# The last expert block's results kept in SBUF and added in the mix through a slot-by-token matrix

## The chip, the cores and the metric

One NeuronCore of one Trainium2 chip runs the whole program; its kernel is written in Bass, with an instruction stream of its own for each of TensorE (PE), VectorE (DVE), ScalarE (ACT), GpSimd (POOL) and SyncE (SP), tied together by semaphores. The metric is the device time of one execution in microseconds, the median over several runs.

## What is computed

Two layers of a diffusion backbone over 256 context tokens and 512 latent tokens of width 1024. Each layer mixes tokens (latent attention, Fourier mixing, neighbourhood attention) and then runs a hierarchical mixture of experts, in float32. The change touches the second part only:

```python
def hier_moe(h, w_rg, b_rg, w_re, b_re, w_gate, w_up, w_down):
    p_grp = jax.nn.softmax((h @ w_rg + b_rg).astype(jnp.float32), axis=-1)
    p_top, g_idx = lax.top_k(p_grp, 1)                      # 1 of 4 groups
    ...
    l_top, e_loc = lax.top_k(e_in, TOP_K)                   # 2 of its 8 experts
    w_tok = (p_top * jax.nn.softmax(l_top, axis=-1)).astype(h.dtype)
    ...
    def expert_block(args):
        xblk, e = args
        return (jax.nn.silu(xblk @ w_gate[e]) * (xblk @ w_up[e])) @ w_down[e]
    yb = lax.map(expert_block, (xb, block_e)).reshape(n_rows, d)
    out = jnp.zeros((t + 1, d), yb.dtype).at[row_tok].add(yb * row_w[:, None])
```

The result goes, scaled by a modulation row, into `ALPHA * x + out` and a layer norm. The first layer does this for 768 tokens (6 tiles of 128), the last one for the 512 latent tokens (4 tiles).

## The kernel before, in words

`NB` = 19 expert blocks of up to 128 slots (a slot is a pair of token and choice) are run in each layer in an order fixed by `expert_blocks` (L150 on). A block serves one expert, two (64 slots each) or four (32 each); which expert stands at which rank is computed on the chip (`of_rank`, `eord`). Blocks 17 and 18, the last two, serve two experts each. `expert_plan` makes a list of steps of it: `rows` (the block's token rows are turned, L1243), `gate`, `up` and `down` in two halves each (`product`, L1230), and `mid` (the product of gate and up is turned, L1253). The last steps are gate 18, mid 17, gate 18, up 18, down 17 (both halves), mid 18, down 18 (both halves).

Expert weights come in packs of 2 MB into `RAW` = 8 slots of SBUF (`raw`). `weight_packs` cuts them: a pack is one whole matrix of one expert, or, where `in_halves` says so, the same half of two experts' matrices. `in_halves` is true for the last block's down weights: pack 94 is the first half of both experts, pack 95 the second, while packs 92 and 93 are the whole down matrices of block 17's two experts, and both are needed before its first half product. A layer has 96 packs. SP issues them in order (L3010), each as soon as the last product that used its slot is done. Behind them on SP's queue stand the rows of the norm (`ln_g`, `ln_b`, in layer 0 two modulation rows as well), which wait for pack 92 to be used.

A block's result lies in PSUM (`slot[1]`); ACT copies it (layer 0, L2513), or DVE scales it (layer 1, L2110), into `yb[i % 2]`, and POOL writes its rows with an indirect DMA to `y_rows` in DRAM (`result`, L2711), one row for each pair of token and choice. When the last two blocks' stores have landed (`y_stored`), POOL raises `y_out`, and SP loads the two rows of each token, tile by tile, into `yg` (L3088); `yg[0]` lies over `yb`. The mix (L700) is then a product with a diagonal matrix for each of the two choices (`share[n][k]` = identity times the token's weight):

```python
for half in range(2):
    for k in range(2):
        last = pe.matmul(slot[n % 2][:, half * 512:(half + 1) * 512], share[n][k],
                         yg[n % 4][k][:, half * 512:(half + 1) * 512], start=(k == 0), stop=(k == 1))
```

A float32 `matmul` leaves two records on PE in the trace. In layer 1 the mix of 4 tiles is followed on DVE by `last_sum` (L1410), the moments, `last_centre` and `last_scale`, and by the output DMAs. In layer 0 tiles 0 to 3 are mixed behind the experts, and tiles 4 and 5 among the first projections of layer 1; DVE goes from `merge_first` (L1379) through `merge_last` to the next norm, and PE turns the normed tiles (L821) and multiplies (L772).

Ahead of the experts DVE computes each pair's slot. `place[k]` (L2044) is a matrix of tokens by slots for choice k that is one where the token's pair has that slot in its block.

`cst` holds constants, its last 1536 columns the position tables (`C_COS`, `C_SIN`), loaded once.

Of the kernel before, what the change touches and what calls it, by code (L numbers as in the profile page):

```python
# [70 lines left out]
C_KCOL, C_RANK, C_HALF, C_CAP, C_ALL, C_NEXT = (C_KROW + NE + k for k in range(6))  # L71
C_BLOCK = C_NEXT + 1
# [20 lines left out]
def shape_constants():  # L93
# [21 lines left out]
    c[:NE, C_NEXT] = np.where(e < DOUBLE, P * e - P, 0)  # L115
    b = np.where(e < hot, e, np.where(pair, hot + (e - hot) // 2, hot + PAIRED // 2 + (e - cold) // 4))
# [93 lines left out]
def program(nc, a, out):  # L210
# [9 lines left out]
    with ExitStack() as ctx:  # L220
# [49 lines left out]
        rk = sb("rk", [P, 464])  # L270
# [110 lines left out]
        idsT = rk[0:NE, 336:464]  # L381
# [20 lines left out]
        yg = [[ar(kb, D), ar(kb + 4, D)] for kb in (128, 136, 144, 80)]  # L402
# [244 lines left out]

        def blocks_to(L, i):

            return sum(1 for k in range(NB) if k % 2 == i % 2) * L + i // 2 + 1  # L650
# [10 lines left out]
        def _(pe):  # L661
# [31 lines left out]
            def mix(L, n):  # L693
# [134 lines left out]
            for L in range(DEPTH):  # L828
# [65 lines left out]
                def latent_value(t):  # L894
                    pe.wait_ge(act_taken, mark["latent", L, t])
                    if t == 0:
                        pe.wait_ge(mla_in, 16 * (NLATER + NMLA * (L + 1)))
# [270 lines left out]
                for k in range(2):  # L1168
                    pe.wait_ge(route_p, 4 * L + k + 1)
# [14 lines left out]
                for k, at in enumerate((C_HALF, C_CAP, C_ALL, C_NEXT)):  # L1184
                    pe.matmul(ps[:, 32 + 32 * k:64 + 32 * k], cst[0:NE, at:at + 1].to_broadcast([NE, P]), of_rank,
                              start=True, stop=True)
                close(pe.matmul(ps[0:NE, 160:161], of_rank, cst[0:NE, C_ALL:C_ALL + 1], start=True, stop=True), vgroups)

                def ranked_ids():

                    ps = vec()
                    for k in range(2):
                        pe.wait_ge(route_p, 4 * L + k + 3)
                        for n in range(nq):
# [9 lines left out]
                                    cst[0:NE, C_TOP + NE:C_TOP + 2 * NE], start=True, stop=True), vgroups)  # L1204

# [71 lines left out]
                for step in plan:  # L1277
                    part, i, half = step
                    if part == "rows":
                        rows_turned(i)  # L1280
                        if i == 1:
                            ranked_ids()
                    elif part == "mid":
# [59 lines left out]
        def _(dve):  # L1343
# [150 lines left out]
            for L in range(DEPTH):  # L1494
# [94 lines left out]
                dve.wait_ge(mla_in, 16 * (NLATER + NMLA * (L + 1)))  # L1589
# [416 lines left out]
                dve.tensor_copy(rk[:, 128:256], ps[:, 32:160])  # L2006
                dve.tensor_tensor(xe[0:NE, 1:2], xe[0:NE, 2:3], ps[0:NE, 160:161], ALU.subtract).then_inc(vec_taken, 1)
# [33 lines left out]
                for k in range(2):  # L2041
# [3 lines left out]
                    dve.sem_inc(route_p, 1)  # L2045

# [41 lines left out]
                for step in plan:  # L2088
# [3 lines left out]
                    if part in ("gate", "up") and half == 1:  # L2092
# [5 lines left out]
                        else:  # L2098
# [3 lines left out]
                                          ).then_inc(half_taken, 1)  # L2102
                    if part == "down" and half == 1 and L + 1 == DEPTH:
# [4 lines left out]
                        if blocks_to(L, i) > 1:  # L2108
                            dve.wait_ge(y_stored[i % 2], 16 * (blocks_to(L, i) - 1))
# [7 lines left out]
                def extra_block(j, b, it):  # L2117
                    with dve.If(count > j):
# [12 lines left out]
                        if L + 1 == DEPTH:  # L2131
                            put = dve.tensor_tensor(yb[0], slot[1][:, :], gf_row, ALU.mult)
                        else:
                            put = dve.tensor_copy(yb[0], slot[1][:, :])
# [6 lines left out]
                if L + 1 < DEPTH:  # L2141
                    dve.wait_ge(unit_used, mark["part_done", L, NB - 1, "down"])
                    shares()
# [14 lines left out]
        def _(act):  # L2158
# [16 lines left out]
            for L in range(DEPTH):  # L2175
# [67 lines left out]
                for c, (name, dst, blocks) in enumerate((("f", fT, qb), ("nq", nqT, qb), ("nk", nkT, BLOCKS))):  # L2243
                    hi = f_hi if name == "f" else n_hi
                    for m in range(4):
# [13 lines left out]
                        if name == "nk" and m:  # L2259
                            if m == 1:  # L2260
                                act.wait_ge(mla_in, 16 * (NLATER + NMLA * (L + 1)))
# [232 lines left out]
                for part, i, half in plan:  # L2494
                    if part == "rows":
                        ps = take()
                        act.copy(xT[i % 3][:, 4:KD, :].rearrange("p a b -> p (a b)"), ps[:, :]).then_inc(act_taken, 1)  # L2497
                    elif part == "mid":
# [624 lines left out]
```

## Time and profile before

| | us |
|---|---|
| median of 3 runs | 2656.22 |
| lowest and highest | 2653.99, 2663.89 |
| the profiled execution's own time | 2657.63 |
| its span | 2655.7 |
| PE busy (matmul) | 2451.5 |
| DVE, ACT, POOL busy | 940.9, 662.8, 352.8 |

Times in the trace are microseconds from the start of the span. A busy PE is not PE at its peak: matmuls are pipelined. "issue" in a chain is time in which an engine waited for nothing that the profile shows. The granted clock (PEclk) is 1.00 at 2.4 GHz and 0.50 at 1.2 GHz.

### The profile page before, as it was taken

The page shows a single profiled execution, that of the slowest core. Times are in us where ns is not written, and L with a number is a line of the kernel's source. Part 1 is how long each engine was busy: PE and PEld are TensorE (multiplying, and loading weights), DVE is VectorE, ACT ScalarE, POOL GpSimd, SP SyncE. Part 2 cuts the span into 40 slices and gives each one's busy share as a digit, 9 for nine tenths or more (in the row PEclk, how much of TensorE's full clock was granted, in tenths as well). Part 3 has the DMA queues.
Part 4 walks back from the last instruction along what each step waited for, and adds up shares of the span by engine and source line. Part 5 has one row for each costly group of instructions (what it writes and reads, how often), then busy time and mean ns, then how long its engine had stood idle before and what let it go on. Part 6 is the DMA issues. An engine that isn't in the chain of part 4 may idle for free.

```text
span 2655.7 us, 32991 instructions
## 1 busy us (share of the span) xinstructions
PE 2451.5 (92%) x12867; PEld 1553.1 (58%) x12867; DVE 940.9 (35%) x1791; ACT 662.8 (25%) x1242; POOL 352.8 (13%) x404
## 2 busy tenths in 40 slices
PE   7999999999999888999996999999999898999995
PEld 4768666788888633443332668567888633443332
DVE  3335466622225720000003544566334730111113
ACT  3221345632222210111011521456333200000000
POOL 1241000000112220010001531000011220010002
PEclk9999999999999889999997999999999889999997
DMA  8671000322214599999998471003433799999995
GB/s 283 213 258 48 7 1 12 75 65 69 65 56 166 226 415 423 427 422 425 427 428 308 158 239 48 7 1 74 113 97 110 299 383 424 426 421 425 427 427 196
DMA packets 217916, 603.87 MB, mean 227 GB/s; under 512 B 63280, under 2 KB 139472, under 8 KB 184736
## 3 DMA queue, kind: packets, MB, share of 16 engines
q1 hardware_dynamic: 189794, 526.02, 51.7%
q0 software_dynamic: 24512, 63.13, 6.8%
q10 hardware_dynamic: 3456, 12.58, 1.2%
q8 instruction: 108, 1.77, 0.3%
q14 instruction: 46, 0.38, 0.0%
HBM read 585.17 MB, written 38.16 MB: 235 GB/s over the span
## 4 chain that ended last, share of the span: by engine, by line
PE 72%; DMA 14%; DVE 7%; ACT 3%; issue 3%; POOL 1%; SPq 1%; DVEq 0%; ACTq 0%; POOLq 0%
PE slot L1230 23%; PE abank L772 18%; PE vbank L772 10%; DMA arena<-in_w_up_e 5%; DMA arena<-in_w_down_e 5%; PE slot L955 2%; PE vbank L989 1%; PE vbank L936 1%; DMA arena<-in_w_in 1%; PE slot L1016 1%; PE abank L872 1%; PE slot L700 1%; PE vbank L762 1%; PE vbank L1049 1%; PE abank L969 1%
## 5 line engine op out<-in xcount | busy, mean ns | idle before, releaser
L1230 PE MATMUL slot<-arena 128*64 128x512 f32 (+2 forms) x3264 | 827.3, 616 | 70.5 <-DMA arena<-in_w_up_e 47.6
L1230 PEld LDWEIGHTS slot<-arena 128*64 128x64 f32 (+2 forms) x3264 | 298.1, 147 | 546.3 <-issue 536.2
L772 PE MATMUL abank<-round,round 128*128 128x512 f32 (+1 forms) x1792 | 493.2, 356 | 9.4 <-DVE round L1501 3.7
L772 PEld LDWEIGHTS abank<-round,round 128*128 128x128 f32 x1792 | 318.7, 189 | 73.1 <-issue 15.9
L772 PE MATMUL abank<-hT_low,round 128*128 128x512 f32 (+1 forms) x896 | 318.1, 355 | 0.0
L772 PE MATMUL vbank<-round,round 128*128 128x512 f32 (+3 forms) x1248 | 290.0, 361 | 6.3 <-issue 5.1
L2101 DVE TENSOR_TENSOR arena<-slot,arena 128x512 f32<-128x512 f32 x76 | 52.6, 692 | 657.3 <-ACT arena L2506 377.9
L772 PEld LDWEIGHTS vbank<-round,round 128*128 128x128 f32 x1248 | 215.4, 189 | 41.0 <-issue 8.3
L772 PEld LDWEIGHTS abank<-hT_low,round 128*128 128x128 f32 x896 | 169.0, 189 | 24.0 <-issue 0.5
L1809 DVE TENSOR_TENSOR arena<-vbank,arena 128x512 f32<-128x512 f32 x72 | 43.4, 603 | 291.9 <-PE vbank L772 284.5
L2683 POOL TENSOR_TENSOR arena<-arena 128x512 f32<-128x512 f32 (+1 forms) x48 | 55.9, 1165 | 578.6 <-DVE arena L1809 578.6
L2497 ACT COPY arena<-abank 128x512 f32<-128x512 f32 x38 | 22.3, 586 | 375.8 <-PE abank L1243 375.7
L2434 ACT ACTIVATE arena<-abank,bT 128x512 f32<-128x512 f32 x72 | 44.5, 619 | 272.7 <-PE abank L772 272.7
L955 PE MATMUL slot<-arena 96*128 96x256 f32 (+1 forms) x288 | 102.7, 475 | 3.5 <-ACT arena L2318 1.8
L1713 DVE TENSOR_TENSOR round<-arena,round 128x1536 fp32r<-128x1536 f32 x48 | 89.5, 1865 | 46.1 <-ACT round L2343 46.1
L2705 POOL DMA_INDIRECT arena<-h_rows,ids x34 | 34.8, 1024 | 487.8 <-PE abank L1243 371.8
L772 PE MATMUL slot<-round,round 128*128 128x512 f32 x384 | 91.4, 400 | 0.4 <-DVE round L1781 0.4
L2343 ACT CAST round<-arena 128x1536 fp32r<-128x1536 f32 x48 | 71.1, 1480 | 63.5 <-PE vbank L772 63.5
L2502 ACT COPY arena<-abank 128x512 f32<-128x512 f32 x38 | 21.9, 587 | 254.3 <-PE abank L1253 254.3
L772 PEld LDWEIGHTS slot<-round,round 128*128 128x128 f32 x384 | 74.2, 194 | 16.6 <-issue 0.8
L2326 ACT ACTIVATE arena<-slot,nmx 128x768 f32<-128x768 f32 (+1 forms) x80 | 65.2, 817 | 64.4 <-DVE nmx L1690 64.4
L2711 POOL DMA_INDIRECT y_rows<-arena,ids x34 | 33.9, 997 | 332.4 <-DVE arena L2110 168.8
(335 smaller groups left out, 2862.4 us busy)
## 6 DMA issues: line engine op xcount, KB each, us to landing
arena<-in_w_up_e SPq DMA_DIRECT2D x44, 2048.0 KB, 25.1
arena<-in_w_down_e SPq DMA_DIRECT2D x44, 2048.0 KB, 26.0
arena<-in_w_gate_e SPq DMA_DIRECT2D x40, 2048.0 KB, 26.9
arena<-in_w_gate_e SPq DMA_DIRECT2D x48, 1024.0 KB, 15.2
arena<-in_w_ada POOLq DMA_DIRECT2D x80, 512.0 KB, 5.0
arena<-in_w_up_e SPq DMA_DIRECT2D x40, 1024.0 KB, 17.8
arena<-in_w_down_e SPq DMA_DIRECT2D x40, 1024.0 KB, 30.8
arena<-in_w_in SPq DMA_DIRECT2D x48, 512.0 KB, 4.3
```

Of the source, the lines that this page charges most:

```text
L772: last = pe.matmul(to, x, y, start=(k == 0 and q == 0), stop=(k == len(terms) - 1 and q == 2))
L955: last = pe.matmul(s[:, o:o + nn], qT[h % 2][0:QK, t * P:(t + 1) * P], kT[h % 4][0:QK, o:o + nn], start=True, stop=True)
L1230: last = pe.matmul(to[at, cols], x[:, at], w[:, at_w, :], start=first, stop=final)
L1713: dve.tensor_tensor(gate_halves(u)[1], graw[u % GRAW], gate_halves(u)[0].bitcast(F32), ALU.subtract).then_inc(w_lower, 1)
L1809: dve.tensor_tensor(dst, ps[:, 0:nn], sg[n % 2][:, 0:nn], ALU.mult).then_inc(vec_taken, 1)
L2101: dve.tensor_tensor(am[i % 3], slot[0][:, n % 2 * FE:n % 2 * FE + FE], am[i % 3], ALU.mult).then_inc(half_taken, 1)
L2326: act.activation(PR[i % 2][:, 0:nk], slot[(ib + i) % 2][:, 0:nk], ACT.Exp, bias=nmx[:, k:k + 1], scale=1.0, accum_out=rsum[:, k:k + 1]).th ...
L2343: act.copy(gate_halves(u)[0], graw[u % GRAW]).then_inc(w_upper, 1)
L2434: act.activation(sg[n % 2][:, 0:nn], ps[:, 0:nn], ACT.Sigmoid, bias=bT[:, col:col + 1], scale=1.0).then_inc(act_taken, 1)
L2683: pool.tensor_tensor(dst, dst, sg[n % 2][:, 0:nn], ALU.add).then_inc(pool_sum, 1)
L2705: pool.indirect_dma_start(out=xb[i % 2], out_offset=None, in_=h_d[:, :], in_offset=names(i), bounds_check=2 * TOK - 1, oob_is_err=False).t ...
L2711: pool.indirect_dma_start(out=y_d[:, :], out_offset=names(i), in_=yb[i % 2], in_offset=None, bounds_check=2 * TOK - 1, oob_is_err=False).t ...
```

## The change

1. `in_halves` now holds for the down weights of the last two blocks: pack 92 is the first half of both of block 17's experts, pack 93 the second.
2. Block 18's result is not stored. Its share in the mix is a third product for each half of a tile: `last_at[:, n, :]`, a matrix of 128 slots by 128 tokens that holds a token's weight at its slot of block 18, times `yb[0]`. `yg` moves off `yb`.
3. The matrix is made after the places: DVE finds the pairs whose expert stands in the last block and whose slot lies in it, multiplies their weight into `last_by` and takes it out of `wtok`; PE turns `last_by` (`last_turned`), ACT copies it. Both lie over the position tables, which SP reloads at the start of layer 1.
4. Rows of `y_rows` that no block writes any more are zeroed once, in layer 0, by a DMA from a zeroed row.
5. SP and POOL wait for the stores of blocks 16 and 17; `shares` (DVE, layer 0) comes ahead of block 18's end; extra blocks (none run with these inputs) use `yb[1]`.

```diff
 def in_halves(order, i, part):
     wide = len(order[i][1]) == 4
-    return wide or i == 0 and part != "down" or i == 1 and part == "gate" or i == len(order) - 1 and part == "down"
+    return wide or i == 0 and part != "down" or i == 1 and part == "gate" or i >= len(order) - 2 and part == "down"
...
+        last_at, last_by = (cst[:, o:o + TOK].rearrange("p (a b) -> p a b", a=NTILES) for o in (C_COS, C_SIN))
+        zero_row = ar(168, 256)
...
-        yg = [[ar(kb, D), ar(kb + 4, D)] for kb in (128, 136, 144, 80)]
+        yg = [[ar(kb, D), ar(kb + 4, D)] for kb in (136, 144, 80, 96)]
...
                 if n >= 2:
                     pe.wait_ge(t_ready, before(L) + n - 1)
-                for half in range(2):
+                elif n == 1:
+                    pe.wait_ge(y_ready, NB * (L + 1))
+                halves = [slice(half * 512, (half + 1) * 512) for half in range(2)]
+                for at in halves:
                     for k in range(2):
-                        last = pe.matmul(slot[n % 2][:, half * 512:(half + 1) * 512], share[n][k],
-                                         yg[n % 4][k][:, half * 512:(half + 1) * 512], start=(k == 0), stop=(k == 1))
+                        pe.matmul(slot[n % 2][:, at], share[n][k], yg[n % 4][k][:, at], start=(k == 0), stop=False)
+                if n == 0:
+                    pe.wait_ge(y_ready, NB * (L + 1))
+                for at in halves:
+                    last = pe.matmul(slot[n % 2][:, at], last_at[:, n, :], yb[0][:, at], start=False, stop=True)
                 last.then_inc(mixed, 1)
...
+                pe.matmul(ps[:, 192:224], cst[0:NE, C_LAST:C_LAST + 1].to_broadcast([NE, P]), of_rank, start=True, stop=True)
...
+                def last_turned():
+
+                    pe.wait_ge(route_p, 5 * L + 5)
+                    for lo in range(0, nq, 4):
+                        ps = act()
+                        for n in range(lo, min(lo + 4, nq)):
+                            last = pe.transpose(ps[:, (n - lo) * P:(n - lo + 1) * P], last_by[:, n, :], ident)
+                        close(last, agroups)
...
+                dve.tensor_copy(last_row, ps[:, 192:224])
...
+                link(dve.scalar_tensor_tensor(sel, q32b, 1.0, each(last_row), ALU.is_lt, ALU.mult))
+                for k in range(2):
+                    w = wtok[:, 0:nq, k:k + 1]
+                    link(dve.tensor_tensor(q2, sel, oh[:, k, 0:nq, :], ALU.mult))
+                    link(dve.tensor_reduce(s1[7], q2, AX_X, ALU.add))
+                    link(dve.tensor_tensor(s1[2 + k], s1[7], w, ALU.mult))
+                    link(dve.tensor_tensor(w, w, s1[2 + k], ALU.subtract))
+                for n in range(nq):
+                    put = dve.tensor_scalar(last_by[:, n, :], place[0][:, n, :], s1[2][:, n, :], None, ALU.mult)
+                link(put)
+                for n in range(nq):
+                    put = dve.scalar_tensor_tensor(last_by[:, n, :], place[1][:, n, :], s1[3][:, n, :], last_by[:, n, :],
+                                                   ALU.mult, ALU.add)
+                put.then_inc(route_p, 1)
...
+            pool.memset(zero_row, 0.0)
             pool.memset(rpb_z, NEG).then_inc(rpb_zero, 1)
...
-                    elif part == "down" and half == 1:
+                    elif part == "down" and half == 1 and i < NB - 1:
                         result(i)
...
                 if L:
                     sp.wait_ge(mixed, before(L))
+                    sp.dma_start(cst[:, C_COS:C_END], cst_d[:, C_COS:C_END]).then_inc(mla_in, 16)
...
                 load_bias(0)
+                if L == 0:
+                    sp.dma_start(y_d.rearrange("(p t) (c f) -> p (t c) f", p=P, f=256),
+                                 zero_row.unsqueeze(1).to_broadcast([P, 8 * NTILES, 256])).then_inc(slots_zero, 16)
...
-                for b in range(2):
-                    sp.wait_ge(y_stored[b], 16 * blocks_to(L, NB - 2 + (NB + b) % 2))
+                for i in (NB - 3, NB - 2):
+                    sp.wait_ge(y_stored[i % 2], 16 * results_to(L, i))
                 sp.wait_ge(X["y_out"], count * 1 + 1)
+                sp.wait_ge(groups_done, mark["xt_done", L, NB - 1])
+                sp.wait_ge(unit_used, mark["part_done", L, NB - 2, "down"])
...
+                    elif n == 3:
+                        sp.wait_ge(unit_used, mark["unit_used", L, len(packs) - 2])
                     for k in range(2):
                         sp.dma_start(yg[n % 4][k], y_d[k * TOK + t * P:k * TOK + (t + 1) * P, :]).then_inc(g_in[n], 16)
```

The code is longer by some lines, so a line number of the changed kernel is higher than before: L1230 becomes L1257, L1253 becomes L1280, L700 becomes L714, and the third product is L718. The first place is TensorE from block 17's down product to the mix of the first tile, at the end of layer 1; `raw_in` is a pack's slot, so `raw_in4` to `raw_in7` are packs 92 to 95. Before:

```order
L1230 MATMUL slot<-arena 64x512 [waits raw_in4,raw_in5,y_ready,act_taken]
L1230 MATMUL slot<-arena 64x512 x7
L1230 MATMUL slot<-arena 64x512 [waits raw_in5,raw_in4]
L1230 MATMUL slot<-arena 64x512 x7
L1253 MATMUL abank<-cst,arena 128x128 [waits act_taken,half_taken]
...
L700 MATMUL slot<-arena 128x512 [waits g_in0,share_ready]
L700 MATMUL slot<-arena 128x512 x3
L700 MATMUL slot<-arena 128x512 [waits g_in1]
L700 MATMUL slot<-arena 128x512 x3
```

Of the change:

```order
L1257 MATMUL slot<-arena 64x512 [waits raw_in4,y_ready,act_taken]
L1257 MATMUL slot<-arena 64x512 x7
L1257 MATMUL slot<-arena 64x512 [waits raw_in5]
L1257 MATMUL slot<-arena 64x512 x7
L1280 MATMUL abank<-cst,arena 128x128 [waits act_taken,half_taken]
...
L714 MATMUL slot<-arena 128x512 [waits g_in0,share_ready]
L714 MATMUL slot<-arena 128x512 x3
L718 MATMUL slot<-arena,cst 128x512 [waits y_ready]
L718 MATMUL slot<-arena,cst 128x512
L714 MATMUL slot<-arena 128x512 [waits y_ready,g_in1]
L714 MATMUL slot<-arena 128x512 x3
L718 MATMUL slot<-arena,cst 128x512 x2
```

The first half of block 17's down product waits for one pack in place of two, and every tile has two more products in the mix.

The second place is SP's queue at the same stage, from the down weights of block 17 to the loads of the results. Before:

```order
L3010 ISA [waits unit_used]
L3010 DMA arena<-in_w_down_e 128x4096
...
L2798 DMA arena<-in_ln_g 128x1024 [waits unit_used]
L2798 DMA arena<-in_ln_b 128x1024
...
L3079 REGISTER_ALU [waits y_stored1,y_stored0]
L3088 DMA arena<-y_rows 128x1024 [waits x1_y_out]
L3088 DMA arena<-y_rows 128x1024 x7
```

Of the change:

```order
L3062 ISA [waits unit_used]
L3062 DMA arena<-in_w_down_e 128x2048
L3062 ISA
L3062 DMA arena<-in_w_down_e 128x2048
...
L2846 DMA arena<-in_ln_g 128x1024 [waits unit_used]
L2846 DMA arena<-in_ln_b 128x1024
...
L3132 REGISTER_ALU [waits y_stored1,y_stored0]
L3145 DMA arena<-y_rows 128x1024 [waits unit_used,groups_done,x1_y_out]
L3145 DMA arena<-y_rows 128x1024 x5
L3145 DMA arena<-y_rows 128x1024 [waits unit_used]
L3145 DMA arena<-y_rows 128x1024
```

The wait on `y_stored` is now one for the stores of blocks 16 and 17; the loads are as many and as large as before, and the pair for the fourth tile waits for the first half of block 18.

## Rows read from the trace of the kernel before

**Rows 1.** Page, part 2: DMA busy tenths and GB/s in 40 slices.

```profile
DMA  8671000322214599999998471003433799999995
GB/s 283 213 258 48 7 1 12 75 65 69 65 56 166 226 415 423 427 422 425 427 428 308 158 239 48 7 1 74 113 97 110 299 383 424 426 421 425 427 427 196
```

**Rows 2.** Chain of waits, last 90 us: start, length (us), what.

```profile
2569.17 26.55 DMA arena<-in_w_down_e
...
2611.43 1.24 DVE arena L2110
...
2613.43 2.52 DMA y_rows<-arena,ids
...
2616.04 0.33 SPq L3088
...
2622.19 10.15 PE slot L700 x16
```

**Rows 3.** Chain of waits at the end of layer 0.

```profile
1422.16 4.62 DMA y_rows<-arena,ids
...
1427.27 0.43 SPq L3088
...
1434.69 9.98 PE slot L700 x16
...
1463.85 2.04 issue
...
1475.27 3.43 PE slot L700 x8
```

**Rows 4.** Windows: engines' busy us, then clock, DMA share, GB/s.

```profile
955.00:960.00 5.00, 5.00 (x45) 2.94 (x46) 3.32 (x12) 0.59 (x1) 0.00 (x0) 1.00 0.97 406
...
2608.00:2609.00 1.00, 1.00 (x6) 0.31 (x4) 0.00 (x0) 0.00 (x0) 0.00 (x0) 1.00 0.27 90
...
2614.00:2615.00 1.00, 0.00 (x0) 0.00 (x0) 0.00 (x0) 0.00 (x0) 0.40 (x1) 0.82 0.07 29
...
2628.00:2629.00 1.00, 1.00 (x3) 0.39 (x2) 0.00 (x0) 0.00 (x0) 0.00 (x0) 0.85 0.05 20
```

**Rows 5.** Timeline, PE: block 17's down product, layer 0 and layer 1.

```profile
1404.57 7.09 PE L1230 MATMUL slot<-arena 128*64 128x512 f32 x32 [1.03 <-DMA arena<-in_w_down_e]
...
2595.85 7.09 PE L1230 MATMUL slot<-arena 128*64 128x512 f32 x32 [3.59 <-DMA arena<-in_w_down_e]
```

**Rows 6.** DMAs issued at 2558.48, 2570.2 and 2577.6: KB, us to landing.

```profile
arena<-in_w_down_e SPq DMA_DIRECT2D x1, 2048.0 KB, 32.3
...
arena<-in_w_down_e SPq DMA_DIRECT2D x1, 1024.0 KB, 30.5
...
arena<-in_w_down_e SPq DMA_DIRECT2D x1, 1024.0 KB, 27.9
```

**Rows 7.** Stores issued at 2604.97, 2578.98 and 1413.48: us to landing.

```profile
y_rows<-arena,ids POOLq DMA_INDIRECT x1, 4.9
...
y_rows<-arena,ids POOLq DMA_INDIRECT x1, 10.8
...
y_rows<-arena,ids POOLq DMA_INDIRECT x1, 7.9
```

**Rows 8.** Timeline, DVE: sums of the third and fourth tile, layer 1.

```profile
2636.51 1.22 DVE L1410 SCALAR_TENSOR_TENSOR arena<-x_sb,slot 128x1024 f32<-128x1024 f32 x1
...
2640.49 1.21 DVE L1410 SCALAR_TENSOR_TENSOR arena<-x_sb,slot 128x1024 f32<-128x1024 f32 x1
```

**Rows 9.** Timeline, DVE: from the last place on, layer 0.

```profile
943.14 0.96 DVE L2044 TENSOR_TENSOR place<-cst,arena 128x768 bf16<-128x768 f32 x1
948.02 0.69 DVE L2101 TENSOR_TENSOR arena<-slot,arena 128x512 f32<-128x512 f32 x1 [3.91 <-ACT arena L2506]
954.25 0.69 DVE L2101 TENSOR_TENSOR arena<-slot,arena 128x512 f32<-128x512 f32 x1 [5.55 <-PE slot L1230]
```

**Rows 10.** Timeline, POOL: the memset ahead of the first loads' signal.

```profile
2.46 0.20 POOL L2575 MEMSET arena<- 128x128 f32 x1
```

More of the change, by code:

```diff
@@ L70 @@
 C_KROW = C_TOP + 64
-C_KCOL, C_RANK, C_HALF, C_CAP, C_ALL, C_NEXT = (C_KROW + NE + k for k in range(6))
-C_BLOCK = C_NEXT + 1
+C_KCOL, C_RANK, C_HALF, C_CAP, C_ALL, C_NEXT, C_LAST = (C_KROW + NE + k for k in range(7))
+C_BLOCK = C_LAST + 1
 C_SIDE = C_BLOCK + NID - FIXED // 2
@@ L115, in shape_constants @@
     c[:NE, C_NEXT] = np.where(e < DOUBLE, P * e - P, 0)
+    c[[r for _, r in expert_blocks()[-1][1]], C_LAST] = 1.0
     b = np.where(e < hot, e, np.where(pair, hot + (e - hot) // 2, hot + PAIRED // 2 + (e - cold) // 4))
@@ L269, in program @@
         eord = sb("eord", [P, 1], I32)
-        rk = sb("rk", [P, 464])
+        rk = sb("rk", [P, 496])
         masks16 = sb("masks16", [P, 2 * P], BF16)
@@ L646, in program, with results_to, mla_by @@
         MOD_AT = ("rows", 6, 0)
+        def results_to(L, i):
+            return sum(1 for k in range(NB - 1) if k % 2 == i % 2) * L + i // 2 + 1
+        def mla_by(L):
+            return 16 * (NLATER + NMLA * (L + 1) + L)
         def blocks_to(L, i):
@@ L1168, in _ @@
                 for k in range(2):
-                    pe.wait_ge(route_p, 4 * L + k + 1)
+                    pe.wait_ge(route_p, 5 * L + k + 1)
                     for n in range(nq):
@@ L1282, in _ @@
                             ranked_ids()
+                            last_turned()
                     elif part == "mid":
@@ L2102, in _ @@
                                           ).then_inc(half_taken, 1)
+                    if part == "down" and half == 1 and i == NB - 1 and L + 1 < DEPTH:
+                        dve.wait_ge(unit_used, mark["part_done", L, NB - 2, "down"])
+                        shares()
                     if part == "down" and half == 1 and L + 1 == DEPTH:
@@ L2140, in _ @@
                     extra_block(turn * 2 + 2, 0, turn + 1)
-                if L + 1 < DEPTH:
-                    dve.wait_ge(unit_used, mark["part_done", L, NB - 1, "down"])
-                    shares()
                 if L + 1 == DEPTH:
@@ L2497, in _ @@
                         act.copy(xT[i % 3][:, 4:KD, :].rearrange("p a b -> p (a b)"), ps[:, :]).then_inc(act_taken, 1)
+                        for lo in range(0, nq, 4) if i == 1 else ():
+                            ps, hi = take(), min(lo + 4, nq)
+                            act.copy(last_at[:, lo:hi, :].rearrange("p a b -> p (a b)"), ps[:, 0:(hi - lo) * P]
+                                     ).then_inc(act_taken, 1)
                     elif part == "mid":
@@ L2725, in _ @@
                 pool.wait_ge(route_v, 3 * L + 3)
-                pool.wait_ge(slots_zero, 32)
+                pool.wait_ge(slots_zero, 48)
                 for k in range(2):
@@ L3033, in _ @@
                         mod_loads(L + 1)
+                        sp.wait_ge(slots_zero, 48)
                         for v_ in range(2):
@@ L3075, in _ @@
                     extra_block(turn * 2 + 2, 0, turn + 1)
-                for b in range(2):
-                    sp.wait_ge(y_stored[b], 16 * blocks_to(L, NB - 2 + (NB + b) % 2))
+                for i in (NB - 3, NB - 2):
+                    sp.wait_ge(y_stored[i % 2], 16 * results_to(L, i))
                 sp.wait_ge(X["y_out"], count * 1 + 1)
+                sp.wait_ge(groups_done, mark["xt_done", L, NB - 1])
+                sp.wait_ge(unit_used, mark["part_done", L, NB - 2, "down"])
                 if L + 1 < DEPTH:
```

28 lines of the change are left out of this document (14 added, 14 removed).

## The prediction

> **What bounds the kernel now.** Read the profile page first. The span has 2655.7 us, and one line of its 40 slices decides the case: DMA stands at 9 tenths or more through two long stretches, some seven slices of 66.4 us each [rows 1]. These are the two expert stages. Each layer streams 96 packs of 2 MB there, and TensorE mostly waits for them. So inside an expert stage only bytes count, and the change leaves the bytes as they are. What is left to win is outside: the seam behind each stage, where the last weights are in, the last results go out to y_rows, come back, and are mixed.
>
> Read next the chain of waits at the end of the program [rows 2]. It is to be seen as a row of single steps, none beside another: the weights of block 17's down product land, its products and those of block 18 run, DVE scales (L2110), POOL stores (2.52 us to landing), SP issues the loads at 2616.04, and TensorE starts to mix at 2622.19. The same row stands at the end of layer 0 [rows 3]: store at 1422.16, 4.62 us to landing, loads from 1427.27, mixing from 1434.69. From block 18's last product to the first mix TensorE does nothing for 10.8 and 14.3 us.
>
> Then the windows of 1 us [rows 4]: 3.2 us after that last product the granted clock falls from 1.0 to 0.5 (from 2.4 to 1.2 GHz), and it is back at full 6.1 us after mixing began. Two tiles are 8 matmuls; they took 10.15 us in the last seam [rows 2], while 4 matmuls (8 records, each fp32 matmul has two) took 3.43 us at full clock [rows 3]. So one matmul of 512 columns costs 0.857 us, eight 6.86, and the fallen clock 3.3 us in the last seam and 3.1 in the other.
>
> **The change part by part.**
>
> *Down weights of block 17 in halves.* TensorE stood idle 3.59 us until block 17's second pack landed, in layer 0 1.03 us [rows 5]. Now pack 92 holds the first halves of both experts, so the first half product needs one pack. It runs in the idle time: begun at 2592.26, 3.55 us long (half of 7.09), and the second half starts when pack 93 is in (2569.17 + 26.55 = 2595.72) and ends at 2599.4 in place of 2602.94. Gain 3.5 us, in layer 0 1.0 us. Block 18 cannot follow so fast, since it waits for bytes now: its packs landed at 2570.2 + 30.5 = 2600.7 and 2577.6 + 27.9 = 2605.5 [rows 6]. Its first half ends at 2604.4, the second runs from 2605.6 to 2609.2, 2.2 us earlier than now, and its scaled result is ready at 2610.5.
>
> *Block 18's result stays on chip.* The seam now waits for the store of block 17, not of block 18. DVE ends its scaling at 2600.65, POOL issues 0.75 us later, at 2601.4 (block 18's own steps are the pattern: 1.24 and 0.76 us in [rows 2]). How long until it lands is the unknown of this case. Stores landed in 2.52 us with the DMA engines empty [rows 2], in 4.9 us under the tail of the traffic, in 10.8 us in full traffic; block 17's in layer 0 took 7.9 us with 2 MB queued beside it [rows 7]. Ends of the range: 2.5 and 10.8. The nearest rows are the 4.9 and the 7.9, for the same store of the same block: one landed at 2609.9, about 1 us after the window in which traffic stopped [rows 4], the other at 1421.4. I take "when the traffic is over, and 1 us". The traffic is the rest of the weights and the two broadcasts for the norm; the latter are now issued half a product earlier, right behind the weights, which closes a gap of about 2 us and lets all end near 2607. The store lands at 2608.0 (6.6 us).
>
> *Loads and mix.* From the landing it is 0.1 us to SP's first load and 6.15 us from there to the mix (2616.04 to 2622.19): start at 2614.25, 7.9 us earlier. TensorE has been idle for 5.0 us then, more than the 3.2 after which the clock fell, so I let it fall and pay 3.3 us again. Against this stand two new matmuls for each tile: 6 x 0.857 = 5.14 us where it was 3.43. DVE needs 4.0 us for a tile (2636.51 to 2640.49 [rows 8]), so the tail was DVE's and is now TensorE's: all 24 matmuls end at 2614.25 + 20.6 + 3.3 = 2638.1, and the fourth tile's sum on DVE, which began at 2640.49, begins then. **Gain at the end: 2.4 us.** What follows it is unchanged.
>
> *The same in layer 0.* The store is issued 1.03 us earlier (1412.45) and lands 7.4 us later at 1419.9 by the same rule (its traffic ends 1.5 us earlier). From landing to mix it was 1434.69 - 1426.78 = 7.9 us, the bias broadcast among it: start at 1427.8. Two tiles are now 12 matmuls, 10.3 + 3.1 us, done at 1441.2 in place of 1444.67: 3.5 us. Here DVE's chain of norms follows, so tiles 2 and 3 have room. Tile 4's two extra matmuls (1.7 us) fit into the 2.04 us in which TensorE then waits; tile 5's (L700 x8, 3.43 us) stand in a stretch where TensorE is without a gap, and cost 1.7 us [rows 3]. **Net 1.8 us.**
>
> *What I cost at nothing.* DVE gets 21 (layer 0) or 17 small steps behind the last place, about 5.6 us as I estimate; the last place ended at 944.1 and DVE's next work began at 948.02, so block 0's gate product slips by some 2 us, and DVE is idle for 5.55 us behind it [rows 9]. The transposes (6, 4 in layer 1) and ACT's copies delay block 1 by about 1.3 us; the DMA share there is 0.97 [rows 4], and packs land 24 us and more after their issue [rows 6], so the queue covers it. If it were short, this would cost its 1.3 us in each layer. The zero fill of y_rows is 6.3 MB, 15 us at 427 GB/s; SP puts it behind the first bias loads, in the fifth slice, and slices five and six carry 7 and 1 GB/s [rows 1]. Without that cover it would cost its 15 us. The reload of the position tables (0.8 MB, 2 us) goes ahead of the dft table on SP's queue, in a stretch where the DMA engines are far from full. The shares on DVE move ahead of block 18's end and were hidden behind its store already. The memset of the zero row stands ahead of the signal for the first loads: 0.2 us by the memset beside it [rows 10], on the path.
>
> Sum: 2.4 + 1.8 - 0.2 = 4.0 us. The profiled execution took 2657.6 us (span 2655.7) and would take 2653.6; the median of the three runs stands 1.4 us below it, so I forecast 2652 us. About 0.5% (13 us) is what a measurement here tells from no change; the runs of before alone spread over 10 us.
>
> **The rivals.**
>
> *The store gets its share at once.* Then block 17's store needs its empty-engine time and its own 0.5 MB a second time, 2.5 + 1.2 = 3.7 us. For it speaks the 4.9 us of [rows 7]; against it the 10.8, at the same size. It would land at 2605.1, the loads would queue behind the broadcasts until 2607, mixing starts at 2612.2, 3.0 us after TensorE's last product, and the clock would hold: end at 2632.8, gain 7.7. In layer 0 (4.62 + 1.2) mixing starts near 1426.2: net 3.4. Together 10.9 us: 2645. The Trainium skill (DMA: Bandwidth & Descriptors, Queues, rings and completion order) says this: each engine takes turns between the queues that have work, packet by packet. The 10.8 us does not fit that rule; the 4.9 us does not rule it out.
>
> *The new wait is worse than the old (slower).* SP waits for a store in full traffic where it waited for one with the engines empty. At 10.8 us it lands at 2612.2, mixing starts at 2618.4 and ends at 2642.3, 1.9 us later than now, since eight more matmuls stand in the tail. In layer 0 it lands at 1423.25, two tiles are done at 1444.6, and tile 5 costs its 1.7: 1.6 us later. With the memset 3.7 us: 2660. It decides itself at a landing time of about 9 us, in both layers.
>
> *The halves do not bring block 17 forward.* If the first halves land no earlier than both packs did, the store stays at 2604.97 and 1413.48 with 4.9 and 7.9 us. Mixing then starts at 2616.1 and 1429.3; gains 0.5 and 0.3, less the memset: 2655.6. Against it: pack 92 is issued 10.7 us ahead of pack 93 [rows 6].
>
> **How the numbers follow.** Forecast 0.45, share at once 0.2, worse wait 0.2, halves idle 0.1, and 0.05 for something that I cost at nothing. Their times are 2652, 2645, 2660 and 2655, each with 2 or 3 us of scatter of the median; the range 2643 to 2661 leaves out about 0.15. Only the outer part of the second case lies beyond 0.5%: faster 0.05, same 0.92, slower 0.03.
>
> **What would show it.** TensorE's idle before block 17's down product is gone, and 1 to 3 us appear before the last half of block 18. The issue row of block 17's store gives its time to landing: 6 to 8 us is my case, under 5 the second, over 9 the third. The windows between the last product and the mix show whether the clock fell. The last chain reads TensorE (24 matmuls), not DVE, up to the fourth tile's sum. I am wrong if the expert stage itself is longer or shorter by more than 3 us, or if a wait for y_ready shows up ahead of the new matmuls.

## The result and the profile after

| | us |
|---|---|
| before, median of 19 runs on the same chips | 2651.99 (2646.83 to 2663.89) |
| after, median of 19 runs | 2660.35 (2655.18 to 2668.66) |
| ratio after / before, 95% interval | 1.0031 (1.0024 to 1.0038) |
| profiled execution of after, its span | 2668.66, 2666.9 |

The change costs 8.4 us, where the forecast was a gain of 4 us below the profiled execution. The direction is certain, the size below the 0.5% that was called "same". Before's median moved too: it was 2656.22 from three runs and is 2651.99 from nineteen. Both profiled executions lie above their medians (by 5.6 and 8.3 us), so their ends are compared below by stretches, not by their spans.

The slices (page, part 2; they answer to [rows 1]) look as forecast: both expert stages at 9 tenths, and one new figure, 101 GB/s in the fifth slice, the zero fill.

```profile
PEclk9999999999999789999998999999999989999998
DMA  8671301322215599999997461003433799999994
GB/s 281 207 264 48 101 1 13 79 71 62 60 56 182 238 373 422 427 422 425 428 426 308 171 236 48 7 1 78 109 95 121 295 375 424 426 422 426 425 426 179
```

The chain of waits at the end of after (it answers to [rows 2]; start, length, what) shows where the case turns:

```profile
2609.59 6.53 DMA y_rows<-arena,ids
...
2616.34 0.34 SPq L3145
2616.68 0.05 issue
2616.73 4.63 DMA arena<-y_rows
2621.36 7.41 issue
2628.76 5.85 PE slot L714 x8
```

The store of block 17 lands, SP loads at once, pair 0 is in at 2621.36 as it should be, and then come 7.41 us of "issue": time in which TensorE waited for nothing that the view shows. The chain of before has the same line, only short:

```profile
2616.43 4.72 DMA arena<-y_rows
2621.14 1.05 issue
2622.19 10.15 PE slot L700 x16
```

TensorE's own timeline (start, length, operation, idle before and its releaser; it answers to [rows 5]):

```profile
2589.30 14.25 PE L1257 MATMUL slot<-arena 128*64 128x512 f32 x64
2603.90 3.65 PE L1257 MATMUL slot<-arena 128*64 128x512 f32 x16 [0.35 <-DMA arena<-in_w_down_e]
...
2613.78 3.65 PE L1257 MATMUL slot<-arena 128*64 128x512 f32 x16 [1.02 <-DMA arena<-in_w_down_e]
2628.76 5.42 PE L714 MATMUL slot<-arena 128*128 128x512 f32 x7 [11.33 <-issue]
```

The idle 3.59 us before block 17's down product are gone (0.35 us is left between its halves), 1.02 us stand before block 18's second half. Between block 18 and the mix TensorE is idle 11.33 us; it was 10.8 [rows 2]. The windows of 1 us (they answer to [rows 4]) add the clock:

```profile
2618.00:2619.00 1.00, 0.00 (x0) 0.00 (x0) 0.70 (x1) 0.00 (x0) 0.00 (x0) 1.00 0.90 328
2619.00:2620.00 1.00, 0.00 (x0) 0.00 (x0) 0.00 (x0) 0.00 (x0) 0.00 (x0) 0.75 0.95 385
2620.00:2621.00 1.00, 0.00 (x0) 0.00 (x0) 0.00 (x0) 0.00 (x0) 0.00 (x0) 0.50 1.05 422
...
2628.00:2629.00 1.00, 0.24 (x1) 0.27 (x2) 0.00 (x0) 0.00 (x0) 0.00 (x0) 0.50 0.24 98
...
2633.00:2634.00 1.00, 1.00 (x3) 0.39 (x2) 0.00 (x0) 0.00 (x0) 0.00 (x0) 0.92 0.00 0
```

It falls from 2.4 to 1.2 GHz 2.1 us after the last product (3.2 us in before) and is back 4.4 us into the mix (6.1 in before). VectorE's first and fourth sum (they answer to [rows 8]) stand 15.4 us apart, 5.1 us a tile; in before they stood 11.5 us apart, the last two of them 4.0:

```profile
2636.44 1.22 DVE L1438 SCALAR_TENSOR_TENSOR arena<-x_sb,slot 128x1024 f32<-128x1024 f32 x1 [17.75 <-PE slot L718]
...
2651.82 1.22 DVE L1438 SCALAR_TENSOR_TENSOR arena<-x_sb,slot 128x1024 f32<-128x1024 f32 x1 [1.15 <-PE slot L718]
```

What TensorE does in the 11.33 us stands in no group of busy time, because branches are not counted as busy. One has to ask for the line of its loop over the extra blocks (`with pe.Fori(0, NX // 2)`, L1332, now L1360). Before, layer 1, the view of one line (duration in ns min/median/max, first and last start), and then layer 0:

```profile
L1332 PEldq COMPARE_BRANCH  x10: 83/216/221, 2611.7 to 2621.9; - x10
...
L1332 PEldq COMPARE_BRANCH  x10: 83/220/230, 1423.1 to 1433.3; - x10
```

After, layer 1 and layer 0:

```profile
L1360 PEldq COMPARE_BRANCH  x10: 83/221/226, 2618.2 to 2628.5; - x10
...
L1360 PEldq COMPARE_BRANCH  x10: 82/221/226, 1426.4 to 1436.8; - x10
```

Ten turns with nothing to do in them: two tests for an extra block and the loop's own branch, three branches of some 0.22 us each and a few register operations. From the first turn's end to the tenth's it is 10.2 to 10.4 us, 1.14 us a turn. The first turn is longer. TensorE's sequencer (PEq or PEldq in the views) entered the loop at 2615.0, 2.4 us before block 18's last product ended (2617.43), and one test in that turn took 2.44 us:

```profile
L1328 PEldq COMPARE_BRANCH  x21: 208/215/2444, 2614.6 to 2628.2; - x21
```

So the first turn ended at 2618.4 and the tenth at 2628.6, and the mix starts at 2628.76. In before the loop was entered at 2608.3, 3.1 us before the last product ended, and left at 2622.0; the mix started at 2622.19. **So in before the loop already ended the wait in layer 1, 0.9 us behind the landing of pair 0; in layer 0 it ended 1.2 us ahead of it.**

That leaves two questions, which the traces alone don't settle: whether it is the loop, or TensorE's instructions arriving late by DMA behind the new traffic, and whether the rest of the change (places, zero fill) costs something too. VectorE's rows stand 6.4 us later than before's at 927 us (927.44 for 921.04), in the router of layer 0, and 10 us later behind the added steps (957.80 for 948.02).

### The profile page after: what moved, and what is told of

Its sections match the earlier page's. It is cut to its first block and busy times, and to the rows that moved or that the text cites. A ratio compares the mean times of both kernels' runs of the same rounds, so it can differ in the third digit from the quotient of the medians.

```text
span 2666.9 us, 33159 instructions
## 1 busy us (share of the span) xinstructions
PE 2471.2 (93%) x12921; PEld 1566.1 (59%) x12921; DVE 951.0 (36%) x1831; ACT 664.0 (25%) x1245; POOL 349.1 (13%) x403
## 5 line engine op out<-in xcount | busy, mean ns | idle before, releaser
L1257 PE MATMUL slot<-arena 128*64 128x512 f32 (+2 forms) x3264 | 825.3, 613 | 65.3 <-DMA arena<-in_w_up_e 41.9
L1257 PEld LDWEIGHTS slot<-arena 128*64 128x64 f32 (+2 forms) x3264 | 298.4, 146 | 538.9 <-issue 524.2
L789 PEld LDWEIGHTS abank<-round,round 128*128 128x128 f32 x1792 | 318.0, 189 | 72.0 <-issue 14.3
L2297 ACT ACTIVATE arena<-abank,bT 128x512 f32<-128x512 f32 (+3 forms) x48 | 25.2, 543 | 204.1 <-PE abank L789 204.1
## 6 DMA issues: line engine op xcount, KB each, us to landing
arena<-in_w_gate_e SPq DMA_DIRECT2D x48, 1024.0 KB, 12.8
```

Of the source, the lines that this page charges most:

```text
L789: last = pe.matmul(to, x, y, start=(k == 0 and q == 0), stop=(k == len(terms) - 1 and q == 2))
L1257: last = pe.matmul(to[at, cols], x[:, at], w[:, at_w, :], start=first, stop=final)
```

## The experiments

All ratios are to before, run on the same chip, with 95% intervals. The chips differ by 1 or 2 us (before's medians beside the runs were 2650.78, 2650.91, 2651.44 and 2652.42), so runs of different groups are better compared by their ratios. To read the seams without the scatter of what runs ahead of them, this table takes from each trace the end of block 18's down product and counts from there: to the first matmul of the mix (the third product, in third_first and third_kept), and to VectorE's first read of the fourth mixed tile. The fourth is the last one in layer 1; in layer 0 two more follow, and the sixth is read 16.8 to 17.0 us behind the fourth in every run but pair0_first and change_skip_pe (19.7 and 19.8).

| run | median us | ratio | layer 0: mix, fourth tile | layer 1: mix, fourth tile |
|---|---|---|---|---|
| before | 2651.99 | 1 | 14.4, 41.7 | 10.8, 29.1 |
| after | 2660.35 | 1.0031 | 12.0, 42.3 | 11.3, 34.4 |
| halves_only | 2648.24 | 0.9986 | 12.5, 39.4 | 9.7, 26.9 |
| prep_only | 2647.99 | 0.9984 | 12.6, 39.4 | 9.8, 26.9 |
| loads_past | 2673.19 | 1.0079 | 17.6, 47.3 | 16.5, 40.2 |
| pair0_first | 2662.10 | 1.0039 | 12.7, 42.7 | 11.2, 34.3 |
| before_skip | 2650.50 | 0.9993 | 11.2, 38.4 | 9.8, 27.5 |
| halves_skip | 2645.95 | 0.9981 | 13.4, 40.2 | 9.7, 26.9 |
| halves_skip_b | 2645.82 | 0.9977 | 12.8, 39.9 | 9.6, 26.3 |
| change_skip | 2647.36 | 0.9985 | 6.1, 36.6 | 4.0, 27.5 |
| change_skip_pe | 2646.06 | 0.9977 | 8.7, 38.9 | 5.3, 27.8 |
| third_first | 2640.37 | 0.9953 | 1.8, 35.1 | 1.4, 22.3 |
| before_turns15 | 2661.38 | 1.0038 | 19.6, 46.0 | 14.0, 30.8 |
| third_kept | 2660.13 | 1.0029 | 11.9, 42.3 | 11.5, 34.9 |

**1. The parts of the change apart: halves_only, prep_only.** The first is before with one line:

```diff
-    return wide or i == 0 and part != "down" or i == 1 and part == "gate" or i == len(order) - 1 and part == "down"
+    return wide or i == 0 and part != "down" or i == 1 and part == "gate" or i >= len(order) - 2 and part == "down"
```

> The kernel before with its down weights of block 17 in halves and nothing else. If the halves are worth what the trace of the change shows for them (block 17's product starts its first half without an idle stretch and ends 3.3 us earlier in layer 1 against the offset of the stage, 7.9 to 4.6 us), and nothing of it is lost behind, the end comes 1 to 4 us earlier: about 2649, ratio 0.9985 to 0.9995. If the bytes bound block 18 all the same, its store and the mix do not move: ratio 1.000.

The second is after with the old seam:

```diff
-                    elif part == "down" and half == 1 and i < NB - 1:
+                    elif part == "down" and half == 1:
                         result(i)
...
-                for i in (NB - 3, NB - 2):
+                for i in (NB - 2, NB - 1):
                     sp.wait_ge(y_stored[i % 2], 16 * results_to(L, i))
...
-                    link(dve.tensor_tensor(w, w, s1[2 + k], ALU.subtract))
+                    link(dve.tensor_tensor(s1[7], w, s1[2 + k], ALU.subtract))
...
-                for at in halves:
-                    last = pe.matmul(slot[n % 2][:, at], last_at[:, n, :], yb[0][:, at], start=False, stop=True)
```

> The changed kernel with all of its preparation (zero fill, matrix, transposes, reload of the tables, halves), but block 18 is stored as before, the loads wait for its store, and the mix has its two products. If the loss is at the seam (late start of TensorE on the mix, third product), this is at the halves' time, ratio to before 0.9985 to 1.000. If the preparation costs the 5 to 8 us by which the changed kernel's expert stages run late in its trace, the ratio is 1.002 to 1.003 and the seam itself is close to neutral.

Measured: 0.9986 (0.9976 to 0.9997) and 0.9984 (0.9973 to 0.9995). The halves gain about 3.7 us (the interval is 0.8 to 6.4), and matrix, transposes, zero fill, reload and memset together cost nothing that these runs resolve, which is 2 or 3 us. So the lateness of after's profiled execution ahead of its seams is not the preparation's: 6.4 us of it were there at 927 us, ahead of the change's first added step on VectorE. It goes with the granted clock, which stood at 0.63 to 0.67 from 900 to 930 us where before's had 1.00 until 920; that the clock is its cause was not tested. The loss, about 12 us against the halves alone, is then made at the two seams; the table shows 10.4 us of it (2.9 in layer 0 and 7.5 in layer 1, halves_only against after).

**2. Loop, or instructions behind the loads: loads_past, pair0_first.** TensorE signals when it has come through the loop (an increment of `share_ready`), and SP holds loads back until then:

```diff
-                pe.wait_ge(share_ready, L + 1)
+                pe.wait_ge(share_ready, 2 * L + 1)
+                pe.sem_inc(share_ready, 1)
...
+                    if n == 0:
+                        sp.wait_ge(share_ready, 2 * L + 2)
```

> The changed kernel, but SyncE issues the y loads only when TensorE has come through the loop over the extra blocks. If TensorE is late because its instructions come by DMA behind the y loads' packets (7.4 us between the landing of pair 0 and the first matmul), it now comes through within 2 to 4 us of its last product, the loads go out at about 2620 to 2621 on the changed kernel's axis, the mix starts 6.2 us after them, and the end is 1 to 3 us earlier than the change's at either seam; ratio to before 1.001 to 1.0025. If the loads themselves are slow or TensorE takes its 10 us anyway, the mix starts 10 us or more after its last product plus the 6.2 us of the loads: 5 us later at each seam, ratio 1.006.

The second holds back pairs 1 and later only (`if n == 1`).

> As loads_past, but pair 0 is loaded at once and only pairs 1 and later wait for TensorE to come through the loop. If the packets ahead of its instructions are what delays TensorE, the mix starts 3 to 6 us earlier than in the changed kernel (gap to its last product 5 to 8 us in place of 11.3), ratio to before 1.000 to 1.002. If not, the gap stays at 11 us and the ratio at 1.003.

Measured: 1.0079 (1.0060 to 1.0097) and 1.0039 (1.0025 to 1.0053). Both fell out against the theory that the y loads delay TensorE's instructions. Loads_past costs somewhat more than the 1.006 that was expected for this case. Its last product, first mix and loads (timelines of PE and SP):

```profile
2614.91 3.65 PE L1257 MATMUL slot<-arena 128*64 128x512 f32 x16 [1.06 <-DMA arena<-in_w_down_e]
2635.03 5.49 PE L714 MATMUL slot<-arena 128*128 128x512 f32 x6 [16.46 <-DMA arena<-y_rows]
...
2630.10 3.85 SPq L3148 DMA_DIRECT2D arena<-y_rows  x8
```

With no load of y_rows under way it is still 11.5 us from TensorE's last product (2618.56) to SP's first load behind the signal. In pair0_first TensorE's idle 11.2 us are put down to its own sequencer, to the signal behind the loop (L1364):

```profile
PE slot L714 <- PEq L1364: 11.2, 1, 11.2
```

**3. The loop taken away: before_skip, halves_skip, change_skip, change_skip_pe.** `count` is the number of extra blocks:

```diff
-                with pe.Fori(0, NX // 2) as turn:
-                    extra_block(turn * 2 + 1, 1, turn)
-                    extra_block(turn * 2 + 2, 0, turn + 1)
+                with pe.If(count > 1):
+                    with pe.Fori(0, NX // 2) as turn:
+                        extra_block(turn * 2 + 1, 1, turn)
+                        extra_block(turn * 2 + 2, 0, turn + 1)
```

and so on every engine (in change_skip_pe on TensorE alone).

> The kernel before, but every engine goes round the loop over the extra blocks (10 turns of 1.1 us, none with work in it) by a branch when there is no such block. In the kernel before TensorE came out of the loop at 2622.0, 0.9 us after pair 0 had landed, in layer 1, and about 1 us before it in layer 0; so at most 1 us is to be had: ratio 0.9990 to 1.000.

> Block 17's down weights in halves, and the loop gone round. Pair 0 landed 0.1 us before the mix in the run with the halves alone, so the loop hides behind the store and the loads there too: 0 to 1 us below the 2648.2 of the halves alone.

> The changed kernel, and the loop gone round on every engine. If the loop is what holds the mix back, the mix starts when pair 0 has landed: 7.4 us earlier in layer 1 (2621.4 in place of 2628.8 on the changed kernel's axis) and 6.3 us earlier in layer 0 (1430.7 in place of 1437.0); less 3 us where the clock falls anyway; 10 to 13 us in all, so about 2648 to 2650, ratio to before 0.998 to 1.000: about level with the halves alone, because the third product of each tile takes back in the mix (5.1 us a tile in place of 4.0 us) what the store gave. If something else delays TensorE (its instructions arriving by DMA behind the loads), the ratio stays at 1.003.

> As change_skip, but only TensorE goes round the loop; VectorE turns in it until 2628.3 (layer 1), where its first sum would be due at about 2629 to 2630. If nothing but TensorE's turns costs, the time equals change_skip's within 1 us; if VectorE is next, it is 1 to 2 us above.

Measured: 0.9993 (0.9982 to 1.0004), 0.9981 (0.9971 to 0.9990), 0.9985 (0.9976 to 0.9995) and 0.9977 (0.9968 to 0.9986). On before the branch is worth nothing that shows; on the changed kernel it is worth 12 to 13 us (2660.35 to 2647.36; by the ratios, 1.0031 to 0.9985, 12.2). PE in change_skip:

```profile
2600.51 3.65 PE L1257 MATMUL slot<-arena 128*64 128x512 f32 x16 [1.06 <-DMA arena<-in_w_down_e]
...
2608.13 6.31 PE L714 MATMUL slot<-arena 128*128 128x512 f32 x8 [3.97 <-DMA arena<-y_rows]
```

Now the mix waits for its data, 3.97 us. With the loop gone the change still gives nothing over the halves alone: 2647.4 against 2646.0, intervals overlapping. In layer 1 the seam shows it: its mix starts 5.7 us sooner after the last product than in halves_skip, yet the fourth tile is read no sooner (27.5 and 26.9). In layer 0 the fourth tile is read 3.6 us sooner (36.6 and 40.2), which the medians do not show; this is left open. The loops of the other engines, kept in change_skip_pe, cost nothing that shows.

**4. The third product: third_first.** change_skip, with block 18's product in front:

```diff
+            def mix_last(L, n):
+
+                for half in range(2):
+                    at = slice(half * 512, (half + 1) * 512)
+                    pe.matmul(slot[n % 2][:, at], last_at[:, n, :], yb[0][:, at], start=True, stop=False)
...
+                if n >= 2:
+                    pe.wait_ge(t_ready, before(L) + n - 1)
+                    mix_last(L, n)
+                elif n == 0:
+                    pe.wait_ge(y_ready, NB * (L + 1))
+                    mix_last(L, 0)
+                    mix_last(L, 1)
                 pe.wait_ge(g_in[n], 32 * (1 + sum(n < len(qtiles(k)) for k in range(L))))
```

> change_skip, and TensorE multiplies block 18's results by their matrix for tiles 0 and 1 before it waits for the y loads, for tiles 2 and later ahead of the other two products. In change_skip TensorE sat idle 4.0 us from its last product to the mix in layer 1, then needed 8.2 us to the first sum and 5.1 us for each tile after it. If the third product is what took back the gain, the first sum comes 2 to 4 us after the mix's start sooner and the second 3.4 us after the first: 3 to 4 us less at the end of layer 1, 2 to 4 in layer 0, so 2640 to 2643, ratio to before 0.996 to 0.9975, the fastest of all. If VectorE's 4.0 us a tile or the last two tiles bound the end anyway, 1 to 2 us: 2645 to 2647.

> The kernel of halves_skip once more, on the same chip as third_first: 2646, ratio 0.998; third_first is to be 3 to 6 us below it if the matrix pays once its product is out of the way, level with it if not.

Measured: 2640.37, 0.9953 (0.9935 to 0.9970), against 2645.82, 0.9977 (0.9967 to 0.9987). This is the fastest of all, 5.5 us below the halves with the branch and 11.1 us below before on the same chip (2651.44), from six runs. PE in third_first:

```profile
2597.71 3.65 PE L1262 MATMUL slot<-arena 128*64 128x512 f32 x16 [1.29 <-DMA arena<-in_w_down_e]
2602.77 3.67 PE L708 MATMUL slot<-arena,cst 128*128 128x512 f32 x8 [1.41 <-DVE arena L2162]
2606.28 7.03 PE L722 MATMUL slot<-arena 128*128 128x512 f32 x16
```

TensorE waits 1.41 us for VectorE's scaling, does both third products while the loads are under way, and goes on without a gap (in layer 0 it then waits 3.40 us for the loads). With this pause of 1.41 us the granted clock stays at 1.00 from 2596 to 2614, and the two tiles' other products take 7.03 us where two tiles took 10.15 [rows 2]. Against change_skip the fourth tile of layer 1 is read 5.2 us sooner: 2.6 us of it are the earlier start (1.4 for 4.0 us), and 2.6 us are saved from there on (20.9 for 23.5 us, the same 24 matmuls, in change_skip with the clock at 0.50 from 2606.4 to 2613.5).

**5. Two checks of the loop's place: before_turns15, third_kept.** Before with `pe.Fori(0, NX // 2 + 5)`, and third_first with its loops.

> The kernel before with five more empty turns of TensorE's loop over the extra blocks (15 in place of 10), nothing else. At 1.12 us a turn TensorE comes out 5.6 us later. If the loop stood level with the store and the loads in the kernel before (0.9 us behind pair 0 in layer 1, 1.2 us ahead of it in layer 0), that costs 5.6 us in layer 1 and 4.4 us in layer 0, 10 us in all: ratio 1.0038. If the loop was well hidden behind them, at most 2 us: 1.000 to 1.001.

> third_first with the loop kept, its ten turns on every engine. TensorE comes out of the loop 11 us after its last product, when all of block 18's results and pairs 0 to 2 are long there, so the third products of tiles 0 and 1 cover no wait: at the change's time, 2659 to 2661, ratio 1.003. If the order of the products by itself were what gained 7 us, the ratio would be 1.000 to 1.001.

Measured: 1.0038 (1.0026 to 1.0050) and 1.0029 (1.0017 to 1.0041). Five empty turns cost before about 10 us. In its trace pair 0 landed at 2622.16 and the chain shows what followed:

```profile
2617.67 4.49 DMA arena<-y_rows
2622.16 4.48 issue
2626.64 8.68 PE slot L700 x16
```

That is the medians' figure; in the traces the mix is 5.2 us later behind the last product in layer 0 and 3.2 in layer 1, for the expected 4.4 and 5.6, and the fourth tile 4.3 and 1.7. The one long test of the first turn accounts for the split. The sequencer entered the loop 3.1 us before the last product ended in both kernels and both layers. In layer 1 the long test took 2.63 us in before, and in this run there was none (its first turn was over at 2610.7, 1.2 us after it was entered); in layer 0 it took 5.06 and 5.77 us. Five turns of 1.14 us, less the 2.4 us that the missing long test saves, are 3.3 us; in layer 0, less the 1.2 us of slack and plus 0.7, they are 5.2. What makes this test long is not shown.

Third_kept is level with the change: where TensorE first turns for 11 us, the order of the products has no wait to fill. Before_turns15 adds turns and no code, so the turns themselves cost time.

## Why the prediction was wrong

- *The halves.* Right. Block 17's wait went (3.59 to 0.35 us), 1.02 us appeared before block 18's second half, and alone they gain 3.7 us (0.8 to 6.4). Block 18's gain of 2.2 us was not measured apart.
- *Block 18's result stays on chip.* Right, and closely. The unknown of the case, the landing of block 17's store in the tail of the traffic, was put at 6.6 us; the row in layer 1 has 6.53, in layer 0 6.7 (forecast 7.4):

```profile
y_rows<-arena,ids POOLq DMA_INDIRECT x1, 6.7
...
y_rows<-arena,ids POOLq DMA_INDIRECT x1, 6.5
```

  Both rivals on this landing (3.7 us, and above 9 us) fell. The rule of turns between queues in the Trainium skill (DMA: Bandwidth & Descriptors, Queues, rings and completion order), by which the first was argued, does not give these 6.5 us by itself.
- *Loads and mix.* **Here it failed, at "6.15 us from there to the mix".** This was read as the time of a load. Its last 1.05 us were "issue", the end of TensorE's loop, whose turns are counted from block 18's last product and not from SP's issue. The start of the mix is the later of two times, pair 0's landing and the end of ten turns; the forecast moved the first by 8 us and carried the second along. The landing did come where it belongs (loads to landing 5.0 us, before 5.1), the mix 7.4 us behind it. The same in layer 0: landing 1430.7, mix 1437.05. Counted from the last product, the mix of layer 1 was forecast at 5.0 us (2609.2 to 2614.25) and came at 11.3; with the loop gone, in change_skip, it came at 4.0. Taking the loop away gave 12 to 13 us back, which is the distance between the forecast gain of 4 us and the measured loss of 8.4.
- *The third product.* Right: 24 matmuls and the fallen clock were put at 23.9 us from the mix's start to the fourth tile's sum, measured 23.06 (2628.76 to 2651.82). Against before the fourth tile of layer 1 is 5.3 us later from the last product, 0.5 of it in the start and the rest from there on. In layer 0 the fourth tile is 0.6 us later and the sixth 0.8. The clock did not keep the 3.2 us that the prediction carried over from before: it fell 2.1 us behind the last product. So "the clock would hold" over 3.0 us of idle, in the case of the store that gets its share at once, is not borne out either.
- *What was costed at nothing* costs nothing that shows (prep_only). VectorE's 21 added steps, estimated at 5.6 us, took 5.8 (952.14 to 957.9).
- *"A row of single steps, none beside another"* was the error behind the error, and with it "TensorE does nothing for 10.8 and 14.3 us": its sequencer was turning. The chain of waits shows the path that ended last. In layer 1 that was the loop itself, unnamed in 1.05 us of "issue"; in layer 0 it was the loads, and the loop ended 1.2 us ahead of them.
- The rival on the slower side had the right size (2660) from a mechanism that did not occur. None of the rivals named TensorE's own arrival.

Put right, the account is this. The halves give 3.7 us. Against them the earlier loads give nothing, since the loop bounds the mix: against halves_only its start, counted from the last product, is 0.6 us sooner in layer 0 and 1.7 us later in layer 1, where after's first turn held a long test and that of halves_only none. From the start to the fourth tile's read the third products and the clock cost 3.5 and 5.8 us. These seams' 10.4 us are about 12 in the medians. The medians also show more than the seams in loads_past (12.7 and 10.9 us above after) and before_turns15 (9.0 and 6.0 above before); why is left open, and the intervals are 3 us wide or more.

With the loop gone, change_skip is 3.6 us below before on its chip, close to the forecast 4. The agreement is within the scatter and does not show each term: the halves with the branch stand as low without the matrix.

## What to carry to other kernels

Before a wait is shortened, look for what the waiting engine itself does meanwhile: ask the trace for its branches and register operations, which no busy time counts, and treat a short "issue" behind a landing as the end of a second path. A loop with a fixed count around conditional work costs its turns even when all of them are empty; one branch around it cost nothing that shows in the medians. Work that needs only what is already on chip goes ahead of the wait, not behind it: here, with the loop out of the way, that made the same matrix worth 5.5 us instead of nothing (third_first against halves_skip_b), and with the loop kept the loss of the change stayed (third_kept).

## What was not expected of the hardware

An empty turn of TensorE's sequencer costs 1.14 us, with compare-and-branch at 0.21 to 0.23 us. The Trainium skill (Advanced Engine Details and Errata, Control Flow Timing) gives about 0.11 us for one, so a turn of three would be an estimated 0.33 us and ten turns some 3 us; the trace has twice that for each branch and 10.2 us or more for the ten, and the measurement decides. On the other engines the same tests of the same loop are shorter: 45 ns on SP, ACT and POOL and 56 on VectorE in before. VectorE's, at the same stage:

```profile
L2118 DVEq COMPARE_BRANCH  x21: 56/56/73, 2612.1 to 2620.1; - x21
```

Their ten turns still take 7 to 10 us (SP's go from 2603.8 to 2613.4).

One branch is often far longer: a test in the first turn took 2.4 to 5.8 us, except in layer 1 of halves_only, prep_only and before_turns15, where none was long, and the one branch over the loop, in the runs without it, took 1.6 to 6.6 us. In third_first, layer 1, it took 3.09 us, hidden behind block 18's product and VectorE's scaling (the view of its line):

```profile
L1365 PEldq COMPARE_BRANCH  x1: 3088/3088/3088, 2598.9 to 2598.9; - x1
```

In layer 0 of the same run it took 4.20 us and ended at 1421.4, 0.6 us behind ScalarE's copy of the results, and TensorE's third product started at 1421.55; by these times the branch came last there.
